# One dot between the tile's product and the weighing, in each of 64 routing steps

## The reference, cut to what matters

```
pre = jnp.einsum('td,thkd->thk', hb, down[ib])      # u_e . h
w   = gb * gelu(pre)
out = jnp.einsum('thk,thkd->td', w, up[ib])
```

## Time and profile before

| | us |
|---|---|
| median of 3 runs | 1694.89 (1690.49 to 1696.66) |
| the profiled execution | 1689.4 |
| span of its profile | 1687.5 |

### The profile page before, as it was taken

One profiled execution on the slowest core, in us unless ns is written; L12 is line 12 of the kernel. 1 busy time (PEld: TensorE's weight loads), 2 busy tenths in 40 slices (PEclk: granted clock), 3 DMA queues, 4 the chain that ended last, 5 costly groups with the idle time before them and its releaser, 6 DMA issues.

```text
span 1687.5 us, 20389 instructions
## 1 busy us (share of the span) xinstructions
PE 1594.6 (94%) x6944; PEld 1168.0 (69%) x6944; DVE 1250.1 (74%) x2389; ACT 552.5 (33%) x1357; POOL 676.0 (40%) x590
## 2 busy tenths in 40 slices
PE   4999999999998999999999999998999998999974
PEld 2887877777886998888888998886444443444431
DVE  6876456778466688999988989998666665676676
ACT  2433145454623622111128888785000000000001
POOL 0000111110002505435776766776744544455464
PEclk8999999999999999999999999999999999999998
DMA  8424421235422438999999999999999999999997
GB/s 342 177 98 175 154 77 60 80 105 199 163 100 88 163 114 306 406 378 378 396 409 369 392 393 385 388 398 354 403 409 409 409 410 411 410 409 409 409 407 288
DMA packets 126280, 499.18 MB, mean 296 GB/s; under 512 B 15456, under 2 KB 15840, under 8 KB 115808
## 3 DMA queue, kind: packets, MB, share of 16 engines
q0 software_dynamic: 75776, 269.52, 41.0%
q1 hardware_dynamic: 50400, 228.35, 35.3%
HBM read 492.04 MB, written 4.72 MB: 294 GB/s over the span
## 4 chain that ended last, share of the span: by engine, by line
PE 33%; DMA 28%; DVE 23%; POOL 6%; issue 4%; ACT 3%; DVEq 2%; SPq 0%; ACTq 0%
DMA ring<-in_up,idx 22%; PE bank L855 8%; DVE ring L1624 7%; PE bank L566 7%; PE bank L568 7%; PE bank L567 7%; POOL ring L1884 6%; DMA ring<-in_down,idx 5%; PE bank L842 2%; DVE accum L1868 2%; DVE acc_ada L1248 1%; DVE att_max L1434 1%; DVEq L1282 1%; ACT prob L938 1%; DVE comb L1449 1%
## 5 line engine op out<-in xcount | busy, mean ns | idle before, releaser
L868 PE MATMUL bank<-stream,wmat 128*128 128x512 f32 x1024 | 443.5, 596 | 10.8 <-DMA stream<-in_up 7.0
L855 PE MATMUL bank<-h2T,stream 128*128 128x256 f32 x2048 | 452.8, 379 | 0.0
L1868 DVE SCALAR_TENSOR_TENSOR accum<-ring,share,accum 128x1024 f32<-128x1024 f32 x243 | 312.1, 1284 | 176.6 <-DMA ring<-in_up,idx 170.3
L1884 POOL DMA_INDIRECT ring<-in_down,idx x256 | 332.5, 1299 | 240.2 <-DVE pre L1624 154.9
L855 PEld LDWEIGHTS bank<-h2T,stream 128*128 128x128 f32 x2048 | 384.2, 190 | 49.5
L868 PEld LDWEIGHTS bank<-stream,wmat 128*128 128x128 f32 x1024 | 195.7, 191 | 258.0 <-issue 246.2
L1884 POOL DMA_INDIRECT ring<-in_up,idx x256 | 269.7, 1054 | 234.1 <-DVE accum L1868 202.5
L1624 DVE CUSTOM_DVE_ANT_0 ring<-ring,h2row 128x1024 f32<-128x1024 f32 x256 | 307.4, 1220 | 29.4 <-DMA ring<-in_down,idx 24.5
L566 PE MATMUL bank<-hT_hi,whi 128*128 128x512 f32 (+1 forms) x504 | 189.2, 375 | 12.1 <-DVE hT_lo L1319 9.5
L568 PE MATMUL bank<-hT_hi,wlo 128*128 128x512 f32 (+1 forms) x504 | 184.4, 366 | 0.0
L567 PE MATMUL bank<-hT_lo,whi 128*128 128x512 f32 (+1 forms) x504 | 184.0, 365 | 0.0
(11 more groups left out here) (233 smaller groups left out, 1831.8 us busy)
## 6 DMA issues: line engine op xcount, KB each, us to landing
stream<-in_downT SPq DMA_DIRECT2D x128, 512.0 KB
stream<-in_up SPq DMA_DIRECT2D x128, 512.0 KB
raw<-in_ada SPq DMA_DIRECT2D x16, 1024.0 KB, 4.8
raw<-in_w_query SPq DMA_DIRECT2D x16, 1024.0 KB, 4.8
ada_raw<-in_ada SPq DMA_DIRECT2D x8, 1024.0 KB, 16.5
raw<-in_w_xp SPq DMA_DIRECT2D x4, 1024.0 KB, 19.6
raw<-in_w_gateA SPq DMA_DIRECT2D x4, 1024.0 KB, 4.8
raw<-in_w_branchP SPq DMA_DIRECT2D x4, 1024.0 KB, 4.8
```

Source lines behind the costliest of these rows:

```text
L855: last = pe.matmul(bank[:, 4 + i % 2, 0:DT], stream[:, i % RING, k * P:(k + 1) * P], h2T[:, k, GB * P:S], start=(k == 0), stop=(k == KT - 1))
L868: last = pe.matmul(bank[:, 2 * tb + half, :], wmat[:, i, tb * P:(tb + 1) * P], stream[:, (ET + i) % RING, half * S:(half + 1) * S], start= ...
L1868: dve.scalar_tensor_tensor(accum[:, b, :], ring[slot][:, :], share[:, b, k:k + 1], accum[:, b, :], ALU.mult, ALU.add).then_inc(sum_done, 1)
L1884: pool.indirect_dma_start(out=ring[slot][:, :], out_offset=None, in_=table, in_offset=bass.IndirectOffsetOnAxis(ap=idx[:, b, k:k + 1], axi ...
```

## The change

In each step one of the two or three dots is taken between `weigh_tile(i)` and `weigh(q, i)`; the others stay behind `one_hots(q + 1)`. The number of dots of each step, their order among themselves, and the plan of the ring slots are the same.

```
             for i in range(SPREAD_AT, ET):
                 weigh_tile(i)
+                dots(1)
                 for q in quads_at(i):
                     weigh(q, i)
                 for q in quads_at(i + 1):
                     one_hots(q)
-                dots(STEP_DOTS + (i % MORE_DOTS == 0 and len(quads_at(i)) == 1))
+                dots(STEP_DOTS - 1 + (i % MORE_DOTS == 0 and len(quads_at(i)) == 1))
```

## The result

The changed kernel takes 1698.30 us (median of 20 runs, 1694.16 to 1703.99), the kernel before 1692.53 (20 runs, 1688.74 to 1698.17). The ratio is **1.0033, 95% interval [1.0023, 1.0044]**: 0.33% slower, 5.8 us between the medians. The forecast was 1696.5 in a range of 1688 to 1705, 1.6 us slower.

What follows compares the result with a forecast made beforehand. The steps were taken as bound by PE, with DVE and transfers close behind. Halfway between all waits gone (3.1 + 0.8 = 3.9 us faster) and all left (7.1 slower) gave +1.6 us: 1696.5 us, range 1688 to 1705.

Steps and rivals of the forecast that it cites:

- What bounds the kernel: Steps bound by PE, DVE and transfers close behind; 3.1 us lost in six places, two shown with late gathers.
- The one-hots behind the dot: In the steps, weighing and one-hots end later; ten of 63 steps stall, 7.1 us if every gather wait stays.
- the third rival: In the steps, front dots' waits for late gathers reach PE through the one-hots: 12 us slower, 1707; chance 0.13.
- The gathers: In the steps, first gather 0.74 us shorter, second up to 0.8 sooner; half of DVE's 16.2 us waits go.
- The DMA engines' share of 1.00: In the steps, 386 GB/s against 397 in the following stage leaves little room, so only half the waits go.
- The second rival: Transfers bound the stage anyway, 392 GB/s being near 397, so neither order matters: 1694.9; chance 0.12.
- The sum: Whole kernel: halfway between 3.9 us faster and 7.1 slower, +1.6 us, giving 1696.5 us on the median.
- every wait left: 7.1 slower: In the steps, if all gather waits stay, PE's stalls for later one-hots add 7.1 us.
- The gap: After the last routing matrix, PE's 3.87 us wait for DVE's drain: 0.8 shorter if DVE is on time, otherwise nothing.
- the stage behind: The 514.2 us after the steps run on their own transfers and move with the steps' end, neither more nor less.

Runs made afterwards that it cites:

- the light stream: Half the columns of down tiles 64 to 127 not streamed: kernel before 1685.51 us (0.9964 to before), changed kernel 1688.99 us (0.9978 to before).
- TWDHD: Against the kernel before, one dot moved behind the weighing and in front of the one-hots: 1691.38 us, ratio 1.0000.
- THDWD: Against the kernel before, order tile weighing, one-hots, dot, weighing, other dots: 1687.89 us, ratio 0.9967; repeated 1687.05 us, 0.9969.
- The copy: Useless VectorE copy added before the changed kernel's front dot: 1696.63 us (1.0019 to before); with half the columns of down tiles 64 to 127 unstreamed, 1688.99 us (0.9980).
- HWDTD: Against the kernel before, order one-hots, weighing, dot, tile weighing, other dots: 1695.63 us, ratio 1.0027.
- the last order: Against the kernel before, tile weighing, one-hots, dot, weighing, dot; three-dot steps add a dot before the one-hots: 1685.59 us, ratio 0.9961.
- THWDD: Against the kernel before, one-hots moved in front of the weighing, all dots after it, none in front: 1693.59 us, ratio 1.0007.

## Why the prediction was right and where it was not

**What bounds the kernel: held.** The stalls of the steps before are late gathers; with the light stream they go to the last 0.1 us.

**The one-hots behind the dot: held as a mechanism.** A step on time has 1.35 us of room left at the start of the steps and 0.90 us at their end (the one-hots of steps 65 and 124 end that long before PE's next routing matrix). It decides once the front dot's wait and DVE's lateness together pass it, as the third rival said: 1.58 us in the stretch shown, and 20 of the 63 periods over 4.5 us instead of five. What the place of the one-hots is worth can be read from TWDHD against THDWD, with 23 long issues each and near equal waits (13.5 and 12.8 us): 1.0000 against 0.9967, some 0.3%. That is an estimate, since the weighing has changed its place too.

**The gathers: the step that failed.** The forecast took DVE's waits to halve, to 8 us; they rose to 30.6. Two sentences made the half. The first, that the front dot's gather would be issued in 0.94 us, held for 36 of 62 (10 of 62 first dots before). The 25 long ones among the others all begin right behind another issue. The second, that the back dot's gather would find POOL free, failed: 0.36 us after its dot's end the tile weighing of 0.29 us is over and DVE is in the front dot of the next step. 16 long issues begin so, released by a dot directly; the other 39 follow behind another issue, where only 7 of 58 did before. So the number of long issues stayed (55, from 58), but they stand otherwise. Before, no more than two follow one another; after, there are eight trains of three to six, whose issues start 2.12 us apart in the mean, while a dot is wanted every 4.35 / 2.25 = 1.93.

What keeps a train going can be read from the rows. In all fourteen profiles an issue that begins inside a dot ends about 0.81 us after the end of that dot's row (see the last section), and the next one, 0.30 us behind, begins 1.11 us after it. In the changed kernel the next dot is running at that moment: it begins 0.2 us after the row's end where only the tile weighing stands between and DVE waits for nothing, and 1.0 us after it where weighing and one-hots do (1045.26 to 1046.27 in the stretch). The copy moves the 0.2 to 0.55, so the next dot still runs at 1.11. In the order of before, two adjacent dots are followed by the weighings and one-hots of the next step, and there the next issue begins inside none of the dots: the train ends. This is an estimate from the rows of these profiles; no run was made to try it.

The Trainium skill (SBUF — State Buffer, the section "Who interferes with whom") says that a VectorE instruction with two SBUF inputs contends with a GpSimd instruction that reads SBUF, and that the ports they share are an exclusive lock. The traces agree for these gathers: an issue that begins inside a dot lasts by so much longer as the dot still runs, 1.99 us at its start and 1.68 us where it begins 0.35 us into it, and 0.94 us inside the weighing, with one input in PSUM, or on an idle DVE. The same section reports `tensor_tensor` as not stalling a DMA and infers that building descriptors does not need the port's read side; here the one-hots and the tile weighing, which are such instructions, do lengthen an issue, and the measurement decides. I had taken the rule for a reason to be faster. It spoke against this change just as much, at the other end of the step, and I had worked it out for the first gather only.

**How far the trains explain the waits.** Only in part. From a dot's end to the end of the issue that it releases it takes 2.07 us in the mean before and 2.01 after: on the average the slots come no later. What changed as well is who waits: 27 of the 28 waits are those of front dots, which ask for their gather sooner than the first dot of a step did, as the third rival said. With the copy in front and the light stream the trains stayed and the waits fell from 21.7 to 4.6 us, which speaks for the early dot; HWDTD, where the front dot stands behind one-hots and weighing, waited 29.0 us with 51 long issues, which speaks for the long issues. No run takes the two apart, so their shares are not shown.

**The DMA engines' share of 1.00: the wrong reason.** It was the ground for taking half. At 0.93 the waits of the changed order were still 21.7 us, and THDWD and the last order lose only 0.2 to 3.7 us of the periods at 1.00 to 1.01. The second rival, by which neither order would matter, falls with it. In the order of before the share was not without meaning: there the lighter stream took the waits from 16.2 to 3.0 us.

**The sum.** That the forecast of 1696.5 lies within 2 us of the measured 1698.3 is luck: it is the middle of two cases, waits that go and waits that stay, and the waits nearly doubled. The term "every wait left: 7.1 slower" was near the measured 5.8, but it stood for waits that stay. The third rival, given a chance of 0.13, had the mechanism; its price of 12 us was twice what came. It took 14 waits of 1.75 us at front dots; the profile has 27 of 1.1 us. Both parts, the one-hots' place and doubled waits, were at work, and one execution lost up to 17 us in the steps (290.9 - 273.8). The gap (0.4 us shorter, of at most 0.8) and the stage behind (513.3 against 514.2 us) came as said.

**What stays open.** Why THWDD, with no train at all and issues like those of before, waited 31.5 us in its profile while its time was that of before. One profile is one execution (THDWD's two have 12.8 and 6.4 us of waits), the times of before spread over 16 us in 35 runs, and I have no second profile of that order. So a difference of waits between two single profiles is weaker evidence than a ratio. Nor was what ends a train tried by itself: the last order removes the trains and the early lateness at once.

## What to carry to other kernels

When a VectorE instruction releases a buffer that GpSimd refills, look at what VectorE does a third of a microsecond later, for every release in the loop and across its edge: if it is another long instruction on two SBUF operands, the refill's issue is held until that has ended. Put work that reads PSUM, or the producer of what TensorE wants next, between such instructions, and put what TensorE wants ahead of anything that waits for a transfer. Here that order, with no instruction more or less, is worth 0.3 to 0.4%, where the same dot in another place lost 0.3%.

## What the runs showed of the hardware that was not expected

An issue is lengthened only by the instruction inside which it begins, and by that to a fixed point. Of the 1946 gather issues in the 63 periods of the fourteen profiles, 1183 begin inside a VectorE instruction with both inputs in SBUF (a dot, one-hots or a tile weighing). 1075 of them end 0.79 to 0.83 us after the end of that instruction's row. The other 108 took 0.93 to 0.95 us: 81 begin within its first 0.05 us, 27 in its last 0.16 us. The 763 that begin on an idle VectorE or inside an instruction that reads PSUM took 0.93 to 0.97 us. In the last order one that began at 1102.70, inside the weighing, took 0.93 us although a dot ran from 1103.13 on; the next began inside that dot, whose row ends at 1104.35, and ended at 1105.16:

```profile
1102.59 0.62 DVE L1802 TENSOR_TENSOR wmat<-bank,wmat 128x452 f32<-128x452 f32 x1
1103.13 1.22 DVE L1624 CUSTOM_DVE_ANT_0 ring<-ring,h2row 128x1024 f32<-128x1024 f32 x1
```
```profile
1102.70 0.93 POOL L1886 DMA_INDIRECT ring<-in_down,idx  x1 [2.39 <-DVE pre L1624]
1103.94 1.22 POOL L1886 DMA_INDIRECT ring<-in_down,idx  x1 [0.30 <-issue]
```

Those that begin inside the one-hots, a shorter instruction of 0.68 us on SBUF operands, take at most 1.46 us. And a lighter DMA load made the trains worse, not better: 75 long issues at 325 GB/s against 55 at 368, and up to nine in a row against six. That DVE then comes to its dots sooner and more evenly is my reading; it was not tried.
